# Two layers, a diffusion-style block and its filters on one core: the filters' even, odd and low parts change engine, and the modulation sums change place

## What is computed

```
layer 0: h += pool_mixer(rmsnorm(h)); h += swiglu(rmsnorm(h))          # the stage that this change is about
layer 1: h += stick_breaking_attention(rmsnorm(h)); h += swiglu(rmsnorm(h))
final rmsnorm, meta tokens dropped
block 2: mod, mod_c = silu(c) @ w_ada + b, silu(c_ctx) @ w_ada + b     # 6 x 1024 values each; of mod_c 2 x 1024 are used
         x += gate1 * merge(neighbourhood_attention(h), hyena(h)); x += gate2 * swiglu(h2); final rmsnorm
hyena:   for n in (0, 1): z = gate[n] * long_conv(z, filt[:, 0, n], filt[:, 1, n], bias[n])
         filt = (sin-MLP of position) @ w3 * decay                      # 256 taps, 2 directions, 2 orders, 512 channels
```

## Time and profile before

| | us |
|---|---|
| median of three runs | 1039.27 |
| profiled execution: its own time | 1043.13 |
| its span (first to last instruction) | 1041.2 |
| TensorE busy | 990.0 (95%) |
| VectorE busy | 827.5 (79%) |
| ScalarE busy | 565.9 (54%) |
| GpSimd busy | 135.0 (13%) |

### The profile page before, as it was taken

The page is one execution under the profiler, slowest core; times in us unless marked ns, Lnnn a source line. Parts: engine busy times, 40 slices in busy tenths (PEclk is TensorE's granted clock), DMA queues, the critical chain, the costliest instruction groups (busy, mean ns, idle before and its releaser), DMA issues.

```text
span 1041.2 us, 19511 instructions
## 1 busy us (share of the span) xinstructions
PE 990.0 (95%) x7946; PEld 957.2 (92%) x7946; DVE 827.5 (79%) x1370; ACT 565.9 (54%) x1062; POOL 135.0 (13%) x148
## 2 busy tenths in 40 slices
PE   6998998999899998999999999899999999999996
PEld 5998998999888888999999999898999999999996
DVE  7999898787888876799978477888898768767543
ACT  5754444344666665555646435666554466655542
POOL 3104132111000003001301210111100210000001
PEclk9999999999999999999999999999999999999998
DMA  7574565665543423699866532423335445645441
GB/s 235 223 262 172 172 238 206 242 238 186 194 149 122 144 80 121 241 349 322 288 217 246 205 126 89 171 96 130 132 127 197 162 162 192 214 170 194 163 162 41
DMA packets 33882, 192.20 MB, mean 185 GB/s; under 512 B 4976, under 2 KB 6272, under 8 KB 15104
## 3 DMA queue, kind: packets, MB, share of 16 engines
q1 hardware_dynamic: 23440, 157.36, 41.9%
q10 hardware_dynamic: 6912, 25.17, 7.3%
q0 software_dynamic: 3440, 8.42, 2.7%
HBM read 187.78 MB, written 3.15 MB: 183 GB/s over the span
## 4 chain that ended last, share of the span: by engine, by line
PE 64%; DVE 23%; ACT 7%; issue 4%; DMA 2%; POOL 1%; DVEq 0%; ACTq 0%; SPq 0%; POOLq 0%
PE ps L93 63%; DVE wl L70 7%; ACT wh L67 2%; DMA raw<-w 1%; DVE a L70 1%; DVE b L70 1%; DVE fh L70 1%; PE ps L96 1%; DVE natl L70 1%; ACT s L67 1%; DVE s L84 1%; DVE hl L70 1%; DVE junk L84 1%; DVE ada L84 1%; DMA fz<-fz 1%
## 5 line engine op out<-in xcount | busy, mean ns | idle before, releaser
L70 DVE TENSOR_TENSOR wl<-raw,wh 128x1024 fp32r<-128x1024 f32 x281 | 344.8, 1242 | 31.3 <-ACT wh L67 30.9
L67 ACT ACTIVATE wh<-raw 128x1024 fp32r<-128x1024 f32 x286 | 295.7, 1049 | 17.2 <-PE ps L93 8.5
L93 PE MATMUL ps<-xh,wh 128*128 128x256 f32 (+1 forms) x992 | 279.5, 282 | 4.2 <-DVE wl L70 2.7
L93 PE MATMUL ps<-xh,wl 128*128 128x256 f32 (+1 forms) x992 | 277.4, 280 | 0.0
L93 PE MATMUL ps<-xl,wh 128*128 128x256 f32 x992 | 277.3, 280 | 0.0
L93 PE MATMUL ps<-xt,wh 128*128 128x272 f32 (+1 forms) x1120 | 221.3, 292 | 10.9 <-DVE fg L70 7.4
L93 PEld LDWEIGHTS ps<-xt,wh 128*128 128x128 f32 x1120 | 179.8, 191 | 14.5 <-DVE fg L70 8.2
L93 PEld LDWEIGHTS ps<-xh,wh 128*128 128x128 f32 x992 | 187.2, 189 | 5.5 <-issue 2.4
L93 PEld LDWEIGHTS ps<-xh,wl 128*128 128x128 f32 x992 | 187.9, 189 | 0.2
L93 PEld LDWEIGHTS ps<-xl,wh 128*128 128x128 f32 x992 | 187.8, 189 | 0.0
L93 PE MATMUL ps<-xt,wl 128*128 128x272 f32 (+1 forms) x560 | 161.3, 288 | 0.0
(11 more groups left out here) (348 smaller groups left out, 1656.1 us busy)
## 6 DMA issues: line engine op xcount, KB each, us to landing
raw<-w SPq DMA_DIRECT2D x141, 1024.0 KB, 4.9
ada<-ada ACTq DMA_DIRECT2D x37, 512.0 KB, 4.6
cb<-ada ACTq DMA_DIRECT2D x11, 512.0 KB, 3.5
raw<-w SPq DMA_DIRECT2D x4, 512.0 KB, 6.6
spare<-w SPq DMA_DIRECT2D x2, 1024.0 KB, 8.1
spectra<-ev POOLq DMA_DIRECT2D x8, 256.0 KB, 3.7
skew<-rpb POOLq DMA_DIRECT2D x8, 192.0 KB, 3.2
x<-x POOLq DMA_DIRECT2D x2, 544.0 KB, 9.4
```

The lines of the kernel that those rows point to most:

```text
L67: return Issued(self.e and self.e.activation(out, src, func, **kw))
L70: return Issued(self.e and self.e.tensor_tensor(out, a, b, op))
L93: return Issued(self.e and self.e.matmul(out, stat, mov, start=start, stop=stop))
```

## The change

1. The low part of w3 (n = 0, 1) moves from GpSimd to VectorE, at f = 5 and 13 in `between`.
2. The even and odd parts move to VectorE behind the taps (`taps_parts`, f = 6, 8, 14, 16), the low parts of both to VectorE one step later (`taps_low`, f = 7, 9, 15, 17). For tt = 0 the even part now lies in the tile `odd`. GpSimd keeps the stores.
3. The modulation's 64 sums are dealt anew: layer 0's up part 18 before, 9 after; its down part 14 and 17; attention 8 and 7; layer 1's up part 21 and 21; layer 1's down part 3 and 10. A down group there has two sums for d = 3 to 6, and the sums now stand ahead of the context's lines and the low parts.
4. Buffer 6 goes, buffers 7 and 8 come; loads are dealt anew. In layer 1's down part ScalarE makes one cast ahead of the loads.
5. ScalarE's wait at f = 10 goes. GpSimd's load of `rope` also waits for the last modulation sum.

```
 ADA (sums): layer 0's up part now
+ADA = {("up", 0, 2, 0): ((0, 0),), ("up", 0, 2, 1): ((0, 1),), ("up", 0, 10, 1): ((1, 0),), ("up", 0, 11, 0): ((1, 1),),
+       ("up", 0, 13, 1): ((2, 0),), ("up", 0, 18, 1): ((2, 1),), ("up", 0, 19, 1): ((3, 0),), ("up", 0, 21, 0): ((3, 1),),
+       ("up", 0, 21, 1): ((4, 0),)}
+for d, n in enumerate((3, 3, 3, 2, 2, 2, 2)):          # layer 0's down part
...
+ADA.update({("down", 1, d, 0): ((37 + d, 0),) for d in (1, 2)})
+ADA.update({("down", 1, d, 0): ((34 + 2 * d, 0), (35 + 2 * d, 0)) for d in (3, 4, 5, 6)})
+ADA_LOAD = {...  ("up", 1, 21): (38,), ("down", 1, 0): (39,), ("down", 1, 1): (40,),
+            ("down", 1, 2): (41,), ("down", 1, 3): (42, 43), ("down", 1, 4): (44, 45), ("down", 1, 5): (46, 47)}
+ADA_BUF = [0, 0, 0, 5, 0, 5, 8, 0, 5, 8, 0, 5, 8, 7, 7, 7, 1] + [2 + f % 3 for f in range(21)] + [1, 8] * 5
 first_act
-            if f == 10:
-                A.wait_ge(S["w_lo"], ("half", 9))
...
+        for m in ADA_LOAD[("down", 0, -1)]:
+            self.ada_load(A, m)
 first_dve, between(f)
+            if f in (5, 13):
+                self.rest(V, ("w3", f // 8), self.S["w_lo"])
             if f in (6, 8, 14, 16):
                 self.taps_dve(V, f // 14, f in (8, 16))
+                self.taps_parts(V, f // 14, f in (8, 16))
+            if f in (7, 9, 15, 17):
+                self.taps_low(V, f // 14, f in (9, 17))
 first_pool
-        self.rest(G, ("w3", 0), S["w_lo_pool"])
         for n in (0, 1):
-            for tt in (0, 1):
-                self.taps_pool(G, n, tt)
...
-                self.rest(G, ("w3", 1), S["w_lo_pool"])
+    def taps_parts(self, V, n, tt):
+        V.tt(ev[:, :], self.tf[:, :], self.tg[:, :], ALU.add).then_inc(S["filt_v"], ("ev", n, tt))
+        V.tt(self.tf[:, :], self.tf[:, :], self.tg[:, :], ALU.subtract).then_inc(S["filt_v"], ("od", n, tt))
...
+    def taps_low(self, V, n, tt):
+        V.wait_ge(S["filt_a"], ("hs", n, tt))
+        V.tt(hl[:, s], self.even(tt)[:, :], hs[:, s].bitcast(F32), ALU.subtract).then_inc(S["filt_v"], ("hl", n, tt))
+        V.wait_ge(S["filt_a"], ("ds", n, tt))
+        V.tt(dl[:, s], self.tf[:, :], ds[:, s].bitcast(F32), ALU.subtract).then_inc(S["filt_v"], ("dl", n, tt))
...
 layer1_act
+            self.twice_square(A, d)
+            self.casts(A, W.spent(("down", 1, d)), 1)
             for m in ADA_LOAD.get(("down", 1, d), ()):
                 self.ada_load(A, m)
-            self.twice_square(A, d)
             self.casts(A, W.spent(("down", 1, d)))
 layer1_dve
             self.add_x(V, "x", d, M0, TR, ...)
+            self.ada_dve(V, ("down", 1, d))
             if d < 4:
                 self.ctx_dve(V, 2 * d), self.ctx_dve(V, 2 * d + 1)
             self.rests(V, W.spent(("down", 1, d)))
-            self.ada_dve(V, ("down", 1, d))
```

More of the change, by code:

```diff
@@ L116 @@
 ROWS = (96, 96, 80)
[L117 to L129, removed]
@@ new lines @@
+_i = 9
+for d, n in enumerate((3, 3, 3, 2, 2, 2, 2)):
+    parts = [((_i + k) // 2, (_i + k) % 2) for k in range(n)]
+    ADA[("down", 0, d, 0)], ADA[("down", 0, d, 1)] = (parts[0],), tuple(parts[1:])
+    _i += n
+ADA.update({("sb", p, 0): ((13 + (p - 1) // 2, (p - 1) % 2),) for p in range(1, 7)})
+ADA[("sb", 7, 0)] = ((16, 0),)
+ADA.update({("up", 1, f, 0): ((16 + f, 0),) for f in range(1, 22)})
+ADA.update({("down", 1, d, 0): ((37 + d, 0),) for d in (1, 2)})
+ADA.update({("down", 1, d, 0): ((34 + 2 * d, 0), (35 + 2 * d, 0)) for d in (3, 4, 5, 6)})
@@ new lines @@
+ADA_LOAD = {("up", 0, 0): (0,), ("up", 0, 4): (1,), ("up", 0, 12): (2,), ("up", 0, 17): (3,), ("up", 0, 19): (4,),
+            ("down", 0, -1): (5, 6), ("down", 0, 0): (7,), ("down", 0, 1): (8,), ("down", 0, 2): (9,),
+            ("down", 0, 3): (10, 11), ("down", 0, 4): (12,), ("sb", 0): (13,), ("sb", 2): (14,), ("sb", 4): (15,),
+            ("sb", 6): (16,), ("up", 1, 0): (17, 18), ("up", 1, 21): (38,), ("down", 1, 0): (39,), ("down", 1, 1): (40,),
+            ("down", 1, 2): (41,), ("down", 1, 3): (42, 43), ("down", 1, 4): (44, 45), ("down", 1, 5): (46, 47)}
@@ L133 @@
+ADA_LOAD.update({("up", 1, f): (18 + f,) for f in range(1, 20)})
+ADA_BUF = [0, 0, 0, 5, 0, 5, 8, 0, 5, 8, 0, 5, 8, 7, 7, 7, 1] + [2 + f % 3 for f in range(21)] + [1, 8] * 5
 POOLED = (3, 4, 5, 0, 1, 2, 3, 4)
 SIGNALS = ("raw0 raw1 raw2 raw3 raw4 ld_xt0 ld_xt1 ld_xt2 ld_cst ld_band0 ld_band1 ld_band2 ld_x0 ld_x1 ld_pw1 ld_fz "
-           "ld_decay ld_bb ld_mask ld_cb ld_at0 ld_at1 ld_at2 ld_at3 ld_at4 ld_at5 ld_at6 ld_ctx ld_rope ld_cmask ld_skew0 ld_skew1 ld_dftf ld_dftg ld_ksh ld_ks0 ld_ks1 st_kd0 st_kd1 st_out "
+           "ld_decay ld_bb ld_mask ld_cb ld_at0 ld_at1 ld_at2 ld_at3 ld_at4 ld_at5 ld_at7 ld_at8 ld_ctx ld_rope ld_cmask ld_skew0 ld_skew1 ld_dftf ld_dftg ld_ksh ld_ks0 ld_ks1 st_kd0 st_kd1 st_out "
@@ L513, in memory_context @@
         self.ada.append(self.at("ada5", self.off["tf"], 1024)[:, :])
-        self.ada.append(self.at("ada6", self.h0 + 4 * T1 * (FT + 14), 1024)[:, :])
+        self.ada.append(None)
+        self.ada.append(self.at("ada7", self.w0 - 4096, 1024)[:, :])
+        self.ada.append(self.at("ada8", self.off["fg0"], 1024)[:, :])
         self.cacc, self.csq, self.crc = [put(n, TR) for n in ("cacc", "csq", "crc")]
@@ L1148, in taps_dve @@
         if n or tt:
-            V.wait_ge(S["filt_g"], ("dl",) + before)
+            V.wait_ge(S["filt_v"], ("dl",) + before)
         V.wait_ge(S["filt_p"], ("taps", n, tt, 0))
@@ L1159, in taps_dve, with even @@
                 S["filt_v"], ("bias", n))
-    def taps_pool(self, G, n, tt):
-        S, ev, (hs, hl, ds, dl) = self.S, self.evs[tt], self.hsd
-        s = slice(512 * tt, 512 * (tt + 1))
[L1165 to L1177, removed]
+    def even(self, tt):
+        return self.evs[1] if tt else self.odd
+    def taps_parts(self, V, n, tt):
+        S, ev = self.S, self.even(tt)
+        V.wait_ge(S["filt_v"], ("tg", n, tt))
+        if tt == 0:
+            V.wait_ge(S["filt_v"], ("bias", n))
+        elif n:
+            V.wait_ge(S["st_kd1"], ("kd", 0, 1))
+        V.tt(ev[:, :], self.tf[:, :], self.tg[:, :], ALU.add).then_inc(S["filt_v"], ("ev", n, tt))
+        V.wait_ge(S["filt_v"], ("ev", n, tt))
+        V.tt(self.tf[:, :], self.tf[:, :], self.tg[:, :], ALU.subtract).then_inc(S["filt_v"], ("od", n, tt))
+    def taps_low(self, V, n, tt):
+        S, (hs, hl, ds, dl) = self.S, self.hsd
+        s = slice(512 * tt, 512 * (tt + 1))
+        V.wait_ge(S["filt_a"], ("hs", n, tt))
+        V.tt(hl[:, s], self.even(tt)[:, :], hs[:, s].bitcast(F32), ALU.subtract).then_inc(S["filt_v"], ("hl", n, tt))
+        V.wait_ge(S["filt_v"], ("od", n, tt))
+        V.wait_ge(S["filt_a"], ("ds", n, tt))
+        V.tt(dl[:, s], self.tf[:, :], ds[:, s].bitcast(F32), ALU.subtract).then_inc(S["filt_v"], ("dl", n, tt))
     def taps_act(self, A, n, tt):
@@ L1240, in ada_load @@
         elif b == 5:
-            A.wait_ge(S["filt_g"], ("dl", 1, 1))
-        elif b == 6:
-            A.wait_ge(S["w_lo"], ("half", 9))
+            A.wait_ge(S["filt_v"], ("dl", 1, 1))
+        elif b == 7:
+            A.wait_ge(S["proj"], ("down", 0, 7))
+        elif b == 8:
+            A.wait_ge(S["ffn_v"], ("hl", 0, 21))
         elif b:
@@ L1543, in sb_act @@
             weights(p, 1, 0)
-            if p < 7:
-                self.ada_load(A, 17 + p)
+            for m in ADA_LOAD.get(("sb", p), ()):
+                self.ada_load(A, m)
             ath(p, 0)
@@ L2320, in second_pool @@
         G.wait_ge(S["proj"], ("down", 1, 7))
+        G.wait_ge(S["ada_v"], ("sum", 47))
         G.dma(self.rope[:, :], self.ins["rope"]).then_inc(S["ld_rope"], ("load",), by=16)
```

22 lines of the change are left out of this document (9 added, 13 removed).

## The result

The changed kernel took 1031.22 us (median of 4 runs, 1029.38 to 1033.25), the kernel before 1039.74 us (4 runs, 1038.90 to 1042.97) on the same chip. The ratio is 0.990, 95% interval 0.9866 to 0.9935: about 8.5 us faster. The prediction was 1028 us, with a range of 1024.5 to 1034 us; the measured median lies in that range, and just above the 1031 us at which the forecast's own range ended. The profiled execution took 1030.09 us, its span 1028.3 (before 1043.13 and 1041.2).

The account below looks back on a forecast made before the run. VectorE, stretched by GpSimd from 66 to 164 us, was taken to stall TensorE, the busiest engine. Savings of 10.0 + 0.45 + 0.8 = 11.2 us off 1039.3 gave 1028 us, range 1024.5 to 1034, the forecast's own 1025 to 1031.

Parts of the forecast that it names:

- rival D: Layer 1's down part: loads, sums and casts wait for each other in a ring and give time back, 1032 us; 10%.
- C: Layer 0's up part: one long stall stays, most likely the second, behind a late chunk after second w3, 1033 us; 10%.
- VectorE's load, 75.9 us: Layer 0's up part, 66 to 164 us: VectorE's load becomes 91.5 + 13.3 - 9.8 - 19.1 = 75.9 us, against TensorE's 86.7.
- Rival A: Layer 0's up part, 66 to 164 us: VectorE stays the bound and the change is slower, 1048 us; 4%.
- Both long stalls with their slow clock, 10.0 us: TensorE's long stalls in layer 0's up part go, with the slow clock behind them: 3.43 + 3.96 + 1.4 + 1.2 = 10.0 us.
- B: Layer 0's up part: it comes out even; filter steps still overrun the banks, stalls keep most of their size, 1037 us; 8%.
- The 0.92 us stall: Layer 0's up part, TensorE waiting for the MLP's output and w3's low part: 0.45 us saved; bounds 0.92 saved, 0.3 lost.
- The 1.61 us stall: Layer 0's up part, second w3, hanging on a transfer: half saved, 0.8 us; bounds 1.61 saved, 1.6 lost.
- "The lag doesn't grow" at f = 5 to 9: Layer 0's up part: VectorE's added 10.1 us fit into 9 and about 1.9 us of room, so its lag doesn't grow.
- Layer 0's down part and attention, 0: Three sums more in the down part, one fewer in attention: no effect; bounds 1.2 us and 0.5 us gained.
- Layer 1's down part, 0: Seven sums more, 8.5 us, fit into VectorE's idle time there: no effect; bounds 0 and 4 us.
- the last x waits for TensorE: Sign of being right, in layer 1's down part: the last x isn't late; TensorE wants the norm 2.6 us after it.

Follow-up runs that it names:

- e4: The changed kernel plus sixteen GpSimd additions of 512 columns whose result nobody reads; 2.6 us below the kernel before, ratio 0.9963 to 1.0003.
- e5: The changed kernel plus 48 GpSimd fills of 512 columns, which only write; 1032.88 us against the changed kernel's 1032.61 us.
- e6: The changed kernel with w3's two low parts back on GpSimd; 11.9 us faster than the kernel before, ratio 0.9866 to 0.9914.
- e7: The changed kernel with w3's low parts earlier in VectorE's queue, ahead of the gate's scaling at f = 5 and 13; 12.6 us faster than the kernel before.
- r2_after: The changed kernel repeated unaltered, on one chip with the version with w3 earlier; 1032.61 us against 1041.97 us for the kernel before.
- r7_w3_earlier: The changed kernel with w3's low parts earlier in VectorE's queue, run again on one chip with the changed kernel; 1029.54 us, the kernel before 1041.97 us.
- r_after: The changed kernel repeated unaltered; 1032.35 us against 1041.46 us for the kernel before, ratio 0.9900 to 0.9939.

## Why the prediction came out

Its mechanism was right: VectorE lagged because its own work, lengthened by GpSimd's filter instructions, left it no time to spare (e4 and e5 show the lengthening apart from all else), and with less load the long stalls went. The median, 1031.22 us, is another matter: it lies just above the forecast's own 1031, nearer to rival D's 1032 than to 1028, though D didn't happen. The range holds it because it had been widened for C and D. The steps:

- *VectorE's load, 75.9 us.* Measured 85.33 for 95.53 us of TensorE's work; for 86.7 that is 77.4. The parts took 0.69 us, taken 0.68; the stretch went wholly. Rival A is out.
- *Both long stalls with their slow clock, 10.0 us.* Comparing the ends of the same groups in both traces, the offset changes by 5.0 us over the first and 5.8 over the second, 10.8: less the 7.4 us of idle time, the slow clock cost 3.4 us, where the prediction had 2.6. Rivals B and C are out.
- *The 0.92 us stall* fell to 0.61: 0.31, taken 0.45. *The 1.61 us stall* fell to 0.83: 0.78, taken 0.8. The place was right (ScalarE still waits 2.3 us for the load), the half was a choice between bounds, and that it fits so well is luck: in the two repeats the stall is 0.52 and 0.48 us.
- *"The lag doesn't grow" at f = 5 to 9* failed. The prediction weighed w3's place in VectorE's queue against the transfer only for the second w3. For the first, the buffer came free 2.8 us later, VectorE idled 4.17 us, and two stalls, 1.03 us, came that the sum lacks. e6 and e7 show that cause: without it the two stalls are gone. By the head of attention this missing loss and the slow clock's larger gain nearly cancel.
- *VectorE's waits for ScalarE's high parts of the filters, 0*: 0.0 us.
- *Layer 0's down part and attention, 0*: attention begins behind the same 2.02 us.
- *Layer 1's down part, 0, and the ring of loads (rival D)*: one wait of 0.2 us for a load, and TensorE busy 30.00 of 30 us. But a sign that the prediction named for being right, that the last x waits for TensorE, failed: in this profile and its first repeat x comes late, at no cost, since TensorE wants it only later; in the second repeat it waits 0.20 us. What wasn't foreseen is that sums now stand beside GpSimd's norm sums and are stretched: VectorE's groups from 527 to 585 us in the changed kernel,

```profile
L70 DVE TENSOR_TENSOR wl<-raw,wh 128x1024 fp32r<-128x1024 f32 x21 | 26.2, 1291 | 0.8 <-ACT wh L67 0.8
L84 DVE CUSTOM_DVE_ANT_0 ada<-ada,cb 128x1024 f32<-128x1024 f32 x5 | 7.9, 1576 | 0.2 <-DMA ada<-ada 0.2
```

with 1576 ns for five of the ten sums instead of 1220 (the other five, `cb<-cb`, take 1215). It still fits there.

- *From the profile to the median.* The sum of 11.2 us was right for the profiled execution (11.05 by the head of attention), but the medians fell by 8.5, 9.1 and 9.4 us, so 1028 was some 3 us too low. The profiled execution of before, 1043.1, lies at the upper end of that kernel's runs (1038.3 to 1044.6 over all calls). The prediction took the whole gain of that one execution off the median. A likely reason for the difference is that the slow clock behind its stalls, 3.4 us, isn't in every execution; there is one profile of before, and this wasn't shown.

What the prediction didn't ask is whether both halves were needed. They weren't: the deal alone gives 9.2 to 11.5 us, and shorter GpSimd instructions alone 10.3. The filters' move as it was made gives 2.1 alone: it trades 19 us of stretch for 13 of work, leaves the sums in the same periods and makes a buffer late. With w3 earlier it gives 9.3, but of the 7.2 us between the two the profiles of this layer show only 3.0.

## What to carry to other kernels

When an in-order engine is the bound of a stretch, compare its load with the other's in that stretch, then look at each instruction that is moved for what it frees: 2.8 us of delay in freeing a load buffer cost more here (3.1 us between the medians of r2_after and r7_w3_earlier) than the instruction's own 1.2 us. Try each half of a change by itself, since two reliefs of the same stall don't add up. And work that only needs a place can be laid into a stage where the engine idles, even stretched; check there how much of the idle time is left.

## What the runs showed of the hardware

GpSimd's instructions that read SBUF stretch VectorE's beside them, its fills don't: a low part of 128x1024 takes 1.22 us alone and 2.06 beside additions, and a scaling out of PSUM 0.43 either way. An instruction with a single SBUF input was held as well (0.29 to 2.37 us, e6).

The granted clock behind the same idle time differs between executions. TensorE stands 2.02 us at the head of attention in every profile. In the changed kernel's first profile the clock then falls to its 1.2 GHz level, in the profile of before it stays at 2.4; before, then changed kernel:

```profile
279.90:283.30 3.40, 3.24 (x27) 2.99 (x25) 2.25 (x5) 3.35 (x9) 0.00 (x0) 1.00 0.01 2
```
```profile
268.90:272.30 3.40, 3.40 (x18) 3.27 (x17) 1.17 (x4) 3.29 (x9) 0.00 (x0) 0.51 0.00 0
```

Of 14 profiles (before, the changed kernel and the twelve runs) 7 show the fall. The fall costs up to 1.5 us, and there most of it comes back at once: where the clock fell, TensorE's next wait (1.24 us, for ScalarE's `a`) is missing. Falls elsewhere, as one that begins between 380 and 393 us in eight of the profiles, cost 1.5 us or so for good: there the gain over before shrinks by 1.6 us in the first repeat (r_after), which has it, and by nothing in the changed kernel's first profile, which doesn't. Such falls may be much of why runs of one kernel lie 2 to 5 us apart; that wasn't tested.
